# Rows of the split activations 258 elements apart instead of 256, and sx in the stage region

## The reference

```python
def first_block(x, c, ctx, ...):
    x = x + pos_embed_2d(...)
    sh1, sc1, gt1, sh2, sc2, gt2 = split(silu(c) @ w_mod + b_mod, 6)
    ...                                     # the same for ctx, which gives the scan's first states
    parts = split_proj(modulate(rmsnorm(x, norm1_g), sh1, sc1) @ w_in)
    o_lat, _, _ = bidir_gla(q, k, v, la_f, la_b, s_f_ctx, s_b_ctx)
    y = merge_branches(parts, o_lat, ...)   # (gate_fft * y_fft + gate_gla * y_gla) @ w_out
    x = x + gt1 * y
    h2 = modulate(rmsnorm(x, norm2_g), sh2, sc2)
    x = x + gt2 * (square(relu(h2 @ w_mlp_in)) @ w_mlp_out)      # 2048 -> 8192 -> 2048
    return rmsnorm(x, final_norm_g)

def second_block(x, ...):
    u = rms_norm(x, norm_mix_pre) @ w_in                          # 2048 -> 4352
    y = concat([short_conv(u_a), conformer_conv(u_b), pool(u_c)]) @ w_out
    x = x + rms_norm(y, norm_mix_post)
    up = causal_depthwise_conv(rms_norm(x, norm_ffn_pre) @ w_up)  # 2048 -> 11264
    gate, val = split(up)
    return x + rms_norm((silu(gate) * val) @ w_down, norm_ffn_post)
```

## Time and profile before

| | us |
|---|---|
| median of 3 runs (2742.12 to 2752.02) | 2747.23 |
| the profiled execution | 2750.23 |
| its span in the profile | 2748.4 |
| TensorE busy | 2613.0 (95%) |
| TensorE weight loads busy | 2441.1 (89%) |
| VectorE busy | 1684.5 (61%) |
| ScalarE busy | 1160.7 (42%) |

### The profile page before, as it was taken

The page is one execution under the profiler, slowest core; times in us unless marked ns, Lnnn a source line. Parts: engine busy times, 40 slices in busy tenths (PEclk is TensorE's granted clock), DMA queues, the critical chain, the costliest instruction groups (busy, mean ns, idle before and its releaser), DMA issues.

```text
span 2748.4 us, 43152 instructions
## 1 busy us (share of the span) xinstructions
PE 2613.0 (95%) x19216; PEld 2441.1 (89%) x19216; DVE 1684.5 (61%) x2007; ACT 1160.7 (42%) x1297; POOL 11.2 (0%) x24
## 2 busy tenths in 40 slices
PE   7899999999998999999999999849899999999997
PEld 4488799799998999999999999839899889988996
DVE  4265666467787745545555567975666646764664
ACT  3332565344335434434434543323444434443443
POOL 0000000000000000000000000000000000000000
PEclk9999999999999999999999999979999999999999
DMA  9875565478775755555555554424455555555552
GB/s 373 330 250 208 205 215 199 146 254 306 285 275 195 272 182 186 187 186 186 185 184 184 171 202 165 153 77 143 139 173 178 195 175 184 181 198 178 181 178 108
DMA packets 77226, 547.81 MB, mean 199 GB/s; under 512 B 8848, under 2 KB 8976, under 8 KB 12272
## 3 DMA queue, kind: packets, MB, share of 16 engines
q1 hardware_dynamic: 74304, 533.53, 55.4%
q0 software_dynamic: 2448, 11.01, 1.0%
q10 hardware_dynamic: 288, 0.50, 0.1%
HBM read 539.77 MB, written 5.24 MB: 198 GB/s over the span
## 4 chain that ended last, share of the span: by engine, by line
PE 85%; DVE 9%; ACT 3%; DMA 2%; issue 1%; SPq 0%; POOL 0%; DVEq 0%; ACTq 0%
PE acc L278 21%; PE acc L282 21%; PE acc L280 21%; PE acc L298 4%; PE acc L300 4%; PE acc L299 4%; DVE wlo L246 2%; DVE cacc L1339 2%; DMA raw<-in_w_mod 2%; PE acc L335 1%; PE mp L300 1%; PE mp L298 1%; PE mp L299 1%; ACT whi L236 1%; PE mp L365 1%
## 5 line engine op out<-in xcount | busy, mean ns | idle before, releaser
L246 DVE TENSOR_TENSOR wlo<-raw,whi 128x1024 fp32r<-128x1024 f32 x805 | 975.1, 1223 | 789.8 <-ACT whi L236 788.3
L236 ACT ACTIVATE whi<-raw 128x1024 fp32r<-128x1024 f32 x805 | 846.6, 1059 | 1263.7 <-PE acc L282 939.9
L278 PE MATMUL acc<-hh,whi 128*128 128x256 f32 x3552 | 1007.9, 284 | 25.7 <-DVE wlo L246 16.9
L280 PE MATMUL acc<-hl,whi 128*128 128x256 f32 x3552 | 998.5, 281 | 0.0
L282 PE MATMUL acc<-hh,wlo 128*128 128x256 f32 x3552 | 998.5, 281 | 0.0
L278 PEld LDWEIGHTS acc<-hh,whi 128*128 128x128 f32 x3552 | 671.7, 189 | 38.8 <-DVE wlo L246 19.5
L280 PEld LDWEIGHTS acc<-hl,whi 128*128 128x128 f32 x3552 | 671.7, 189 | 1.3 <-issue 1.0
L282 PEld LDWEIGHTS acc<-hh,wlo 128*128 128x128 f32 x3552 | 671.4, 189 | 0.0
L278 PE MATMUL acc<-mh,whi 128*128 128x256 f32 x1536 | 433.6, 282 | 16.8 <-DVE ml L1419 15.1
L282 PE MATMUL acc<-mh,wlo 128*128 128x256 f32 x1536 | 432.4, 282 | 0.0
L280 PE MATMUL acc<-ml,whi 128*128 128x256 f32 x1536 | 432.4, 282 | 0.0
(11 more groups left out here) (307 smaller groups left out, 2144.6 us busy)
## 6 DMA issues: line engine op xcount, KB each, us to landing
raw<-in_w_in SPq DMA_DIRECT2D x98, 1024.0 KB, 5.0
raw<-in_w_mod SPq DMA_DIRECT2D x96, 1024.0 KB, 5.1
raw<-in_w_up SPq DMA_DIRECT2D x88, 1024.0 KB, 4.9
raw<-in_w_mlp_in SPq DMA_DIRECT2D x64, 1024.0 KB, 4.9
raw<-in_w_mlp_out SPq DMA_DIRECT2D x64, 1024.0 KB, 4.8
raw<-in_w_down SPq DMA_DIRECT2D x44, 1024.0 KB, 4.9
raw<-in_w_out SPq DMA_DIRECT2D x32, 1024.0 KB, 4.9
raw<-in_w_fourier_out SPq DMA_DIRECT2D x8, 1024.0 KB, 5.4
```

What stands on the lines that cost most here:

```text
L236: nc.scalar.activation(whi[:, r, :], raw_slot(k)[:, 2 * GC * j:2 * GC * (j + 1)], ACT.Copy)\
L246: nc.vector.tensor_tensor(wlo[:, r, :], raw_slot(k)[:, 2 * GC * j:2 * GC * (j + 1)], whi[:, r, :].bitcast(f32), ALU.subtract).then_inc(S[" ...
L278: nc.tensor.matmul(dst, whi[:, r, cols], hi[:, kt, :], start=begin, stop=False, skip_group_check=True)
L280: nc.tensor.matmul(dst, whi[:, r, cols], lo[:, kt, :], start=False, stop=False, skip_group_check=True)
```

## The change

The tensors hh, hl, mh and ml get rows of PITCH = NT + 2 = 258 elements, of which 256 are in use: row kt begins 1032 x kt bytes behind the tensor's begin in place of 1024 x kt. The two regions that hold them grow from 32768 to 33024 bytes. The names hh, hl, mh and ml stand for views of the first 256 elements of each row, so no code that uses them is changed. ch and cl keep their rows of 256. What lies behind in SBUF moves by 256 (region_a) or 512 bytes (region_x, region_b).

To make room, sx (1024 bytes) becomes one more tenant of the stage region. Since it now lies where post goes, POOL's DMA of post waits for zz_ok (sx has been read) instead of x4_rt.

```diff
+PITCH = NT + 2
...
-        (mrow, cv, posc, macc, stage, _, posc2, post) = overlay(
+        (mrow, cv, posc, macc, stage, _, posc2, sx, post) = overlay(
             "region_s", 8192,
...
             [("hold_macc", [P, 2, GC], f32), ("posc2", [P, 8, 64], f32)],
+            [("sx", [P, NT], f32)],
             [("post", [P, D], f32)])
...
         (hh, hl, xN, gN) = overlay(
-            "region_h", 32768,
-            [("hh", [P, KT, NT], f32r), ("hl", [P, KT, NT], f32r)],
+            "region_h", 8 * KT * PITCH,
+            [("hh_rows", [P, KT, PITCH], f32r), ("hl_rows", [P, KT, PITCH], f32r)],
             [("xN", [P, 2, D], f32), ("gN", [P, 2, D], f32)])
         (ch, cl, lab, keb, tq, state, dft, smid, mh, ml, hf) = overlay(
-            "region_a", 32768,
+            "region_a", 8 * KT * PITCH,
...
-            [("mh", [P, KT, NT], f32r), ("ml", [P, KT, NT], f32r)],
+            [("mh_rows", [P, KT, PITCH], f32r), ("ml_rows", [P, KT, PITCH], f32r)],
             [("hf", [P, KT, NT], f32)])
...
-        sx = sb("sx", [P, NT])
         fss = sb("fss", [P, 3, 2, 4])
+        hh, hl, mh, ml = (rows[:, :, 0:NT] for rows in (hh, hl, mh, ml))
...
-            pool.wait_ge(S["x4_rt"], 1)
+            pool.wait_ge(S["zz_ok"], 1)
             pool.dma_start(post[:, :], ins["post"]).then_inc(S["post_in"], 16)
```

## The result

| | before | change |
|---|---|---|
| median of 6 runs each, us | 2744.68 (2739.15 to 2752.02) | 2758.09 (2754.93 to 2760.93) |
| ratio, 95% interval | | 1.0043 (1.0028 to 1.0057) |
| the profiled execution, its span, us | 2750.23, 2748.4 | 2758.28, 2756.5 |

The changed kernel is slower by 0.43%, a little more than the 0.3% that a measurement of this kernel can tell from no change. The forecast was 2748 us. Where the 12 us (0.43% of the time) come from is to be looked for in small differences.

The account below looks back on a forecast made before the run. TensorE, busy 95%, was taken as the bound through 15264 split 256-column matmuls at 118.7 ns. Terms 0 + 0 + 0 on 2750.23 us, set against the 2747.23 median, gave 2748 us; range 2725 to 2790, no change 0.52.

Parts of the forecast that it names:

- (a): Matmuls of L350 to L352: 64 weight columns pace at 117.1 ns, no less than 117.4 with 128, against colliding streams.
- (b): 512-column matmuls: 233.6 ns is almost exactly twice 117, so the loss grows with the moving columns.
- (c): The 512-column matmuls have exchanged roles and other start offsets, yet pay the same per column.
- (1): TensorE's split matmuls with moved rows: 0 ns each, between bounds of -163 us and +743 us.
- rival A: Moving rows beginning inside a fetch piece touch one more: +14 us, 2762 us with pieces of 4 elements; chance 0.18.
- dearer case: Moving rows fetched in pieces of 8 elements, 12 of 16 rows paying 3.7 ns: +42 us, 2790 us; a third of 0.18.
- Rival B: Changing offsets push all split matmuls into one existing pace, 117.4 or 120.0 ns: at most 20 us either way; chance 0.20.
- C: Offsets were the cost in the split matmuls: pace falls to 108 ns, -163 us, 2585 us; chance 0.06.
- D: Half the moving rows stream at the plain fp32 pace: +743 us, 3491 us; chance 0.04.
- E: The rows stay where they were for the engines: time as forecast, given no chance of its own.
- (2): VectorE's and ScalarE's writes of hi and lo parts in 4 runs of 256: 0, at most +9 us.
- (3): sx in the stage region and post's later DMA: 0 us, post landing at about 2002 us with 697 us to spare.

Follow-up runs that it names:

- e2: The changed kernel with rows 260 elements apart instead of 258, each beginning on a multiple of 16 bytes: 2732.71 us, 0.9943 of before.
- e4: The changed kernel with rows 256 apart, all begun 8 bytes later, and the low parts moved further: 2766.94 us, 1.0071 of before.
- e6: The kernel before with one unused tile of 32 bytes ahead of hh, nothing else: 2713.73 us, 0.9871 of before.
- e1: A kernel of its own, the 256-column matmul stream alone, with varied row distances and shifts of rows, low part or weights: 113.3 to 120.4 ns per matmul.
- e5: The matmul stream alone, rows 256 apart, begun later mostly by multiples of 16 bytes, some settings moving weights too: 113.3 ns per matmul at best, 117.1 unshifted.
- e3: The changed kernel with rows back at 256 apart, keeping only the part with sx and post: 2748.62 us, 1.0005 of before.
- e9: The changed kernel, rows 258 apart, with an unused tile of 32 bytes ahead of hh: 2748.30 us, 1.0000 of before.

## Why the prediction was right and wrong, step by step

**What bounds the kernel: right.** TensorE's pace in the split products decides. Most of what e2, e4 and e6 changed was made of it: with 1.39 ns more (e4), 0.76 ns less (e2, 117.68 in place of 118.44 ns) or 2.36 ns less (e6, 116.08) per matmul, x 15264 gives +21, -12 and -36 us, where the spans moved by +17, -18 and -37.

**Does a row's offset set the pace: wrong, and this is the step that failed.** The prediction concluded from (a), (b) and (c) that the pace belongs to the moving stream itself and not to a meeting of two addresses. e1 and e5 show the contrary: 113.3 to 120.4 ns by nothing but the offset, and back to 117.1 when the weights follow; e6 shows it in the kernel, 35 us by a pad of 32 bytes. Point (a), 64 weight columns being no faster, was a true row and the wrong conclusion: e5 repeats it (22.75 us) and shows that this form just doesn't have the gain at 32 bytes that the 128-column form has. Point (b), 233.6 being twice 117: in e5 the 512-column form goes from 233.6 to between 230.5 and 233.7 ns by its offset, so it too depends on it, and the doubling proves nothing. Point (c), other offsets and the same pace: those offsets happen to have a similar price. All three compared different forms at one offset each; none varied the offset of one form. The trace had no such row, as the prediction said, and the prediction should have given "no change" less than 0.52 for it.

**(1) The matmuls at 0 ns: wrong by about +0.45 ns.** The term is the sum of two effects of several ns by row that nearly cancel in the mean; that it came out near the forecast 0 was luck, since the reason given for the 0 was wrong. The odd rows cost 2.1 ns more than the even ones in the MLP (119.96 against 117.9), where rival A had 1.85 ns for a piece of 4 elements; by A's sum that is +14 us, and rival A's time was 2762 us against 2758.09 measured. Its dearer case (pieces of 8 elements, 2790) did not come: e2, where half of the rows would begin inside a piece of 8, is faster than before. The Trainium skill gives the piece ("SBUF — State Buffer", the note on cachelines: lines of 16 bytes, two hits per line for full bandwidth, a penalty for each access that crosses to a new line), but no price. One line more for a row that begins off a line agrees in its sign with the 120.0 ns of the odd rows and of e4. The prediction's reading of it, one hit on the first and last line, was off: 8 bytes off leaves two elements there; one it would be at 4 bytes off, where e1 has 120.4 in place of 119.4 ns. And rival A is incomplete. By it the rows of e2, all on multiples of 16, would be alike, and they go from 113.3 to 120.0 ns. It leaves the even rows of the change where they were, and they have become 0.8 ns faster in the MLP. Two readings are left for that, and the runs don't separate them: changing distances average over prices like those of e5 (117.4 ns in the mean), or they keep the stream out of the 118.7 ns into which the MLP falls in every trace with rows 256 apart at the old addresses. Alone, changing distances gained nothing (e1: 118.2 ns at 260 elements against 117.1 at 256). At 2300 us the change is slower, because before had fallen into 117.4 ns there. Rival B was right that the engine's fast and slow paces would give way to a single one (843 in all three stretches), and its size, at most 20 us either way, holds; its picture of one of three old paces does not, for 119.0 is a mean over rows of 115.8 to 120.8. C and D did not come, nor E: the pace by kt shows that the rows moved.

The 9.5 ns above the Trainium skill's N / 2.4 + 2.5 ns ("TensorE: Matmul & The Clock Gate", "Back-to-back issue gap", which gives it for an isolated matmul) were not all fixed, either: at the best offset 4.1 are left (113.3). The prediction's own bound of 108 ns rested on a misread row: the program has 64 plain fp32 matmuls at L335 and the trace 128 records of them, in the earlier trace rows 216 ns apart, so one takes two records, 432 ns, and 108 ns is a quarter of it and not a half. That changes no term of the sum. No run came near 108 ns. The same page, in Part 2, gives the moving operand and the weight load a read port each, and I had let that speak against a dependence on offset. It did not hold as an argument: in e1 moving only the weights moves the pace (119.1 in place of 117.1 ns), and the measurement decides.

**(2) The writes at 0: right.** 1226 and 1062 ns, to the nanosecond what they were, and VectorE's 1684.5 us are unchanged.

**(3) sx and post at 0: right.** Post was issued at 2000.2 and landed at 2005.5 us, where I had written about 2002; e3, which is this part alone, has 1.0005 (0.9991 to 1.0019), and no engine waits for post.

**The sum.** 2758.09 us is inside the range of 2725 to 2790 and 10 us above the forecast (by luck, as said under (1)), just outside the 2740 to 2756 that the likeliest case had by itself. Of the checks named, the count of 843 in place of 845 stays within the three that I allowed, since I had looked for it in the MLP only, where the loss is smallest (0.3 ns); the stretch at 2300 us with 843 in place of 854 tells it. A better check would have been the spread by rows of one kt, which A's paragraph did name.

**What stays open.** The same arrangement has not the same pace alone and in the kernel: 117.1 alone and 118.7 (or 117.4) in it for the distance of 256; 118.2 and 117.6 for 260; 113.3 alone, 113.3 and 117.8 in it with the 32 bytes. In the stream alone no weights are loaded or split meanwhile; whether that makes the difference, no run tests. What selects the pace of a stretch, I don't know. It mostly changes behind a gap, and in e6 once, near 656 us, behind two steps of 125 and 123 ns in the middle of a stream. Whether it is banks, a shared port or an arbiter that makes the distance count can't be told from these runs. Of the 8 us between the two spans 3 are not paces but gaps, which differ between runs as well; and the two executions differ by 8 us where the ratio says 12, because the profiled execution of before (2750.23) was one of its slower ones (median 2744.68).

## What to carry to other kernels

Where TensorE's stream is the bound, as here, the addresses of the two operands against each other can be a tuning knob of a per cent (1.3% in this kernel): try a pad of 16, 32, 48, ... bytes in front of the moving rows and measure each in the kernel, for neither the stream alone nor a neighbour's price foretells it. Keep rows at multiples of 16 bytes: with all rows alike, those off it had 119.4 to 120.4 ns alone, those on it 113.3 to 119.6. Compare medians of many runs, since one profile shows one outcome of several paces. To show that something does not depend on an offset, a row is needed in which only the offset differs; equal paces of different forms don't show it.

## What was not expected of the hardware

- A pad of 32 bytes ahead of the moving rows made this kernel 1.3% faster (0.9871), a pad of 64 bytes did nothing (1.0000).
- Alone, the pace of 256-column split matmuls runs from 113.3 to 120.5 ns by the distance of rows and weights modulo 128 bytes; three distances (high rows, low rows, wlo against whi) count, and not additively.
- At one offset the stream has two or three paces, each kept for a stretch (117.4, 118.7 and 120.0 before; 113.3 and 117.8 in e6), and not the same one in each run. With a changing offset the change has 843 or 844 in seven of eight stretches of 100 us (848 in the one from 650 us on). Its 6 runs lie within 6 us and e2's 5 within 4, where before's lie within 9 to 18 us in the four sets; but e9's 12 lie within 11, so that the scatter shrinks by it is not shown.
- Four runs of 256 elements with gaps of 8 bytes cost VectorE and ScalarE exactly as much as one run of 1024 (1226 and 1062 ns).
